# Diagonal scan: product and rounded count on ScalarE, the difference alone on GpSimd

## The reference

```python
mag = jnp.exp(dt * ar)
abar_r, abar_i = mag * jnp.cos(dt * ai), mag * jnp.sin(dt * ai)
...
drive_r = jnp.einsum('bsgh,gph->bsgp', ug, bbar_r)
drive_i = jnp.einsum('bsgh,gph->bsgp', ug, bbar_i)
a_shape = (1, seq, S5_GROUPS, S5_STATE)
elems = (jnp.broadcast_to(abar_r, a_shape), jnp.broadcast_to(abar_i, a_shape), drive_r, drive_i)
_, _, h_r, h_i = lax.associative_scan(_complex_linear_combine, elems, axis=1)
y = (jnp.einsum('bsgp,ghp->bsgh', h_r, c_re.astype(f32))
     - jnp.einsum('bsgp,ghp->bsgh', h_i, c_im.astype(f32)))
```

## Time and profile before

| | |
|---|---|
| median of the runs | 1574.51 us |
| lowest run | 1571.92 us |
| the profiled execution | 1572.47 us, of which the span is 1570.7 us |
| VectorE busy over the span | 1142.6 us, 73% |
| ScalarE busy over the span | 791.3 us, 50% |
| GpSimd busy over the span | 83.2 us, 5%, nearly all of it in the S5 phases |
| S5 phases on GpSimd | 966.5 to 1039.8 us |
| S5 tables on ScalarE | 977.5 to 1072.7 us |
| S5 on VectorE | 977.8 to 1087.6 us |

### The profile page before, as it was taken

The page is one execution under the profiler, slowest core; times in us unless marked ns, Lnnn a source line. Parts: engine busy times, 40 slices in busy tenths (PEclk is TensorE's granted clock), DMA queues, the critical chain, the costliest instruction groups (busy, mean ns, idle before and its releaser), DMA issues.

```text
span 1570.7 us, 22351 instructions
## 1 busy us (share of the span) xinstructions
PE 1467.8 (93%) x8907; PEld 1262.3 (80%) x8910; DVE 1142.6 (73%) x1824; ACT 791.3 (50%) x1079; POOL 83.2 (5%) x82
## 2 busy tenths in 40 slices
PE   5789988999999999999999999889999899999998
PEld 5788765799988889877899888656786578799987
DVE  6798865699876857766886558999985665466653
ACT  4766654455434545444555436547554634354442
POOL 0000000000000000000000003930020000000000
PEclk8999999999999999999999999999999899999999
DMA  9756622678687543336566565333334243245551
GB/s 381 299 202 272 237 101 101 226 297 349 246 340 296 202 161 134 135 122 232 189 239 240 181 217 190 112 108 131 133 134 161 81 161 108 101 161 183 185 195 62
DMA packets 42519, 298.57 MB, mean 190 GB/s; under 512 B 4657, under 2 KB 4913, under 8 KB 7473
## 3 DMA queue, kind: packets, MB, share of 16 engines
q1 hardware_dynamic: 39984, 283.52, 48.6%
q0 software_dynamic: 1568, 8.39, 1.5%
q10 hardware_dynamic: 864, 5.24, 0.9%
HBM read 292.94 MB, written 4.19 MB: 189 GB/s over the span
## 4 chain that ended last, share of the span: by engine, by line
PE 45%; DVE 21%; PEld 15%; ACT 8%; issue 7%; DMA 3%; PEldq 1%; ACTq 0%; SPq 0%; DVEq 0%
PE ps L1038 19%; PE ps L1046 14%; PEld ps L1038 8%; PEld ps L1046 6%; DVE ring_at_lo L1316 6%; ACT w_hi L1305 3%; DMA ring_at<-stream 3%; DVE ring_at L1175 2%; PE ps L1079 2%; PE ps L2626 1%; DVE arena_at L2194 1%; DVE arena_at L3193 1%; PE ps L3096 1%; PE ps L3537 1%; DVE arena_at L3202 1%
## 5 line engine op out<-in xcount | busy, mean ns | idle before, releaser
L1316 DVE TENSOR_TENSOR ring_at_lo<-ring_at,w_hi 128x2048 fp32r<-128x2048 f32 (+1 forms) x218 | 495.9, 2278 | 171.7 <-ACT w_hi L1305 171.2
L1305 ACT ACTIVATE w_hi<-ring_at 128x2048 fp32r<-128x2048 f32 (+1 forms) x218 | 412.3, 1898 | 176.5 <-PE ps L1038 121.1
L1038 PE MATMUL ps<-w_hi,arena_at_lo 128*128 128x512 f32 x1104 | 301.0, 395 | 1.6 <-DVEq L4488 0.8
L1046 PE MATMUL ps<-h_hi,w_hi 128*128 128x256 f32 x1440 | 238.9, 288 | 17.8 <-DVE ring_at_lo L1316 8.3
L1038 PEld LDWEIGHTS ps<-w_hi,arena_at_lo 128*128 128x128 f32 x1104 | 204.8, 188 | 46.1 <-issue 2.7
L1046 PE MATMUL ps<-h_hi,ring_at_lo 128*128 128x256 f32 x1440 | 229.6, 281 | 0.0
L1046 PE MATMUL ps<-hT_at_lo,w_hi 128*128 128x256 f32 x1440 | 229.6, 281 | 0.0
L1046 PEld LDWEIGHTS ps<-h_hi,w_hi 128*128 128x128 f32 x1440 | 199.6, 191 | 26.1 <-issue 16.1
L1046 PEld LDWEIGHTS ps<-hT_at_lo,w_hi 128*128 128x128 f32 x1440 | 196.7, 190 | 0.0
L1046 PEld LDWEIGHTS ps<-h_hi,ring_at_lo 128*128 128x128 f32 x1440 | 196.6, 190 | 0.0
L1038 PE MATMUL ps<-ring_at_lo,arena_at_lo 128*128 128x512 f32 x552 | 170.6, 390 | 0.0
(11 more groups left out here) (464 smaller groups left out, 1646.9 us busy)
## 6 DMA issues: line engine op xcount, KB each, us to landing
ring_at<-stream SPq DMA_DIRECT2D x266, 1024.0 KB, 4.9
arena_at_lo<-kept_hi POOLq DMA_DIRECT2D x4, 1024.0 KB, 7.3
arena_at<-bias ACTq DMA_DIRECT2D x4, 768.0 KB, 6.5
kept<-arena_at POOLq DMA_DIRECT2D x4, 512.0 KB, 4.2
arena_at<-kept ACTq DMA_DIRECT2D x2, 1024.0 KB, 5.8
x_res<-x SPq DMA_DIRECT2D x1, 1024.0 KB, 11.3
arena_at<-mem POOLq DMA_DIRECT2D x1, 1024.0 KB, 12.9
kept_hi<-arena_at_lo POOLq DMA_DIRECT2D x1, 1024.0 KB, 5.1
```

The lines of the kernel that those rows point to most:

```text
L1038: mm = pe.matmul(k.ps[:, bank + t, :], x_tile(f, slice(t * P, (t + 1) * P)), w, start=first and n == 0, stop=last and n == 2)
L1046: mm = pe.matmul(k.ps[:, bank + q // 2, (q % 2) * TOK:(q % 2 + 1) * TOK], w[:, q * P:(q + 1) * P], x, start=first and n == 0 and q % 2 == ...
L1305: act.activation(k.w_hi[:, s % HI, 0:n, :], k.ring[:, c % RING, 0:n, :], ACT.Identity).then_inc(k.hi_done, 1)
L1316: dve.tensor_tensor(k.w_lo[:, c % RING, 0:n, :], k.ring[:, c % RING, 0:n, :], k.w_hi[:, s % HI, 0:n, :].bitcast(F32), ALU.subtract).then_i ...
```

## The change

ScalarE makes the product and the rounded count of a tile by three activations and the new function `counts`: time times turns, the same plus ROUND, and that minus ROUND. The constant ROUND comes as a per-partition operand from two new columns of the constants. GpSimd only takes the difference. `counts(0)` and `counts(1)` come before `tables(0)`, `counts(2)` after it; then `counts(i + 3)` follows `tables(i + 1)` in each step. `n` gets a second buffer, and the waits go by new semaphore counts: GpSimd waits for a tile's three counts, ScalarE for the difference two tiles back before it writes `n` again, and `tables(i)` for difference i.

```diff
+        "rounds": np.broadcast_to([1.5 * 2.0 ** 23, -1.5 * 2.0 ** 23], (P, 2)),
...
-            ("s5_phases", 4 * S5T), ("s5_tables", S5T), ...
+            ("s5_counts", 3 * S5T), ("s5_phases", S5T), ("s5_tables", S5T), ...
...
         def tables(i):
             cos, sn = self.cos[:, i % 3, :], self.sn[:, i % 3, :]
-            act.wait_ge(*m["s5_phases"].at(4 * i + 4))
+            act.wait_ge(*m["s5_phases"].at(i + 1))
...
+        def counts(i):
+            n, r, f = self.n[:, i % 2, :], self.r[:, i % 6, :], self.turns[:, i:i + 1]
+            if i >= 2:
+                act.wait_ge(*m["s5_phases"].at(i - 1))
+            act.activation(r, k.con("time"), ACT.Identity, scale=f).then_inc(m["s5_counts"].sem, 1)
+            act.activation(n, k.con("time"), ACT.Identity, scale=f, bias=k.con("rounds")[:, 0:1]).then_inc(m["s5_counts"].sem, 1)
+            act.wait_ge(*m["s5_counts"].at(3 * i + 2))
+            act.activation(n, n, ACT.Identity, bias=k.con("rounds")[:, 1:2]).then_inc(m["s5_counts"].sem, 1)
+
+        counts(0)
+        counts(1)
         tables(0)
+        counts(2)
         yield
         for i in range(S5T + 3):
             if i + 1 < S5T:
                 tables(i + 1)
+            if i + 3 < S5T:
+                counts(i + 3)
             yield
...
         def phases(i):
-            n, r, f = self.n, self.r[:, i % 6, :], self.turns[:, i:i + 1]
-            if i >= 1:
-                pool.wait_ge(*m["s5_phases"].at(4 * i))
-            if i >= 6:
-                pool.wait_ge(*m["s5_tables"].at(i - 5))
-            pool.tensor_scalar(n, k.con("time"), f, ROUND, ALU.mult, ALU.add).then_inc(m["s5_phases"].sem, 1)
-            pool.tensor_scalar(r, k.con("time"), f, 1.0, ALU.mult, ALU.mult).then_inc(m["s5_phases"].sem, 1)
-            pool.wait_ge(*m["s5_phases"].at(4 * i + 2))
-            pool.tensor_scalar(n, n, 1.0, -ROUND, ALU.mult, ALU.add).then_inc(m["s5_phases"].sem, 1)
-            pool.wait_ge(*m["s5_phases"].at(4 * i + 3))
+            n, r = self.n[:, i % 2, :], self.r[:, i % 6, :]
+            pool.wait_ge(*m["s5_counts"].at(3 * i + 3))
             pool.tensor_tensor(r, r, n, ALU.subtract).then_inc(m["s5_phases"].sem, 1)
...
-    n, r, cos, sn = gla.take(1, TOK)[:, 0, :], gla.take(6, TOK), gla.take(3, TOK), gla.take(3, 2 * TOK)
+    n, r, cos, sn = gla.take(2, TOK), gla.take(6, TOK), gla.take(3, TOK), gla.take(3, 2 * TOK)
```

More of the change, by code:

```diff
@@ L3060, in __init__ @@
         self.m = {n: k.mark(n, c) for n, c in (
-            ("s5_phases", 4 * S5T), ("s5_tables", S5T), ("s5_drive", S5T), ("s5_turned_in", 2 * S5T), ("s5_added_in", S5T),
+            ("s5_counts", 3 * S5T), ("s5_phases", S5T), ("s5_tables", S5T), ("s5_drive", S5T), ("s5_turned_in", 2 * S5T), ("s5_added_in", S5T),
             ("s5_scanned", 2 * S5T), ("s5_turned_out", 2 * S5T), ("s5_c_spread", 4),
```

## The result

The changed kernel takes 1583.97 us in the median of six runs (1578.47 to 1585.27), the kernel before 1570.44 in six runs beside it: a ratio of 1.0084 with a 95% interval of [1.0063, 1.0105]. One of those six was a slow run of 1822.68 us, which the ratio leaves out. Run once more the changed kernel gave 1.0072 [1.0052, 1.0092]. By the ratios it is 11 to 13 us slower; its time lies above the forecast (1573 to 1578) and 1 us above the top of the whole range (1583). The profiled execution took 1584.38 us with a span of 1582.6.

A forecast was written before the change was run, and what follows sets the result against it. VectorE was taken as the bound in the scan (966 to 1090 us). Start +2.7, later place +1.4, clock +0.3, contention -4.0 and subtraction +2.4 make +2.8 us: 1575.5 us forecast, 1573 to 1578 at 0.60, whole range 1570 to 1583.

The forecast's parts named there:

- Elsewhere: Outside the scan's terms: second buffer of `n`, two more constant columns in a load long done, GpSimd's dropped wait; all free.
- Start: Scan's start: counts ahead of the high halves (L1305) delay L1316 and the product of 998.88; +2.7 us, bounds 1.5 and 3.5.
- One later L1305: The L1305 of 1018.16 has only 0.09 us of cover before its L1316; +1.4 us, bounds 0 and 2.9.
- rival 3: ScalarE becomes the bound, L1305 exposed behind every tile's counts: +32 us, 1604 us, over 2% slower; chance 0.02.
- Clock: Scan's output products: both slow ones get about half a microsecond more idle time, +0.3 us.
- the third: Third output product, 1.92 us after 2.88 us idle: falling to 1.2 GHz would cost 1.7 us.
- Contention won: VectorE's scans, turn-outs and sums after 1007 us run faster without three GpSimd instructions per tile; -4.0 us.
- the subtraction kept: GpSimd's subtraction meets VectorE on about 8 later tiles at 0.3 us each; +2.4 us, bounds 0 and 5.3.
- Rival 2: The kept subtraction costs most of what the other GpSimd instructions did: +9.4 us, 1581.9 us; chance 0.14.
- Rival 1: Small gain: subtraction falls beside L1316 or PSUM readers and costs nothing, L1305 of 1018 finds cover; 1571.2 us; chance 0.24.
- the sum by the rule: SBUF port rule: each of 8 kept subtractions costs its whole 0.72 us, 5.8 us instead of 2.4, time 1578.7 us.

The follow-up runs named there:

- padded execution: Profiled run of the changed kernel with 56 unused words ahead of `w_hi`, restoring buffer places within 256 bytes; against the kernel before 1.0031 (1577.64 us).
- mended start: Changed kernel with the first three tiles' product and count left on GpSimd: 1.0049 without pad, 0.9991 with the 56-word pad, against the kernel before.
- padded constants: Kernel before with only the two constant columns and 56 unused words ahead of `w_hi`: 1.0006 [0.9990, 1.0023], 1574.26 us.
- no difference: Changed kernel with the 56-word pad, GpSimd's subtraction left out and `tables` waiting for the counts: 0.9990 [0.9975, 1.0005] against the kernel before, 1571.95 us.
- ScalarE's part alone: Padded kernel, ScalarE's three activations per tile written to an unread buffer, GpSimd doing all four instructions as before: 1.0020 [1.0003, 1.0036], 1575.36 us.
- only the others moved: Kernel before with `w_hi` in place and `h_hi`, `ones` and a small buffer 32 bytes later: 0.9994 [0.9980, 1.0007], 1571.88 us.
- either mending alone: Padded changed kernel with either the first three tiles' counts on GpSimd (0.9991) or the subtraction left out (0.9990), against the kernel before.
- both mendings and pad: Changed kernel with 56-word pad, first three tiles' counts on GpSimd, and counts(i + 3) ahead of tables(i + 1): 0.9984 against the kernel before, 1571.22 us.

## Why the prediction was wrong, step by step

**The step that failed: "Elsewhere ... the constants two more columns in a load long done ... Free".** I costed the columns as a transfer. As a shift of what lies behind them they cost 0.48% [0.30, 0.65] alone, and 0.06% [-0.10, 0.23] with the places restored. Without them the change is at 1.0031, 1577.6 us against 1572.1, inside the range. I had not looked at what lies behind the constants. The prediction also held that only 2%, 31 us, can be told from no change; the intervals here reach some 0.2% to either side.

**The scan's own sum, +2.8 us.** By medians it measured +4.9 us [2.7, 7.2], which includes the forecast. The places of the padded execution, counted from the L1316 of 966.50 to behind the last output product, add up to +6.2 (2.6 + 0.5 - 0.9 + 1.4 - 1.0 + 1.1 + 2.6, within 0.1); I go by those for the terms. That execution is the slowest of its twelve.

*Start, forecast +2.7.* Right. The high halves came 4.3 and 7.2 us late (4.35 and 7.2 forecast) once the 4.17 us are taken off by which ScalarE's instruction just ahead of the counts (975.57 before, 979.74 after) was late already. The first output product came 2.6 us late, with and without pad. What I missed is the first step: `tables(0)` stands behind two counts too, so the first turn-in already waited 2.49 us at 986.61, and the wait at L1317 behind it was shorter for that. From the L1317 of 998.30 to the product VectorE won back 0.6 us (0.75 forecast). The mended start confirms the place: 0.40% less with pad, 0.23% less without.

*One later L1305, forecast +1.4.* Right. L1317 of 1027.88 waits 1.69 us, and the difference grows by 1.4 us there. No other chunk was exposed, so rival 3 is out.

*Clock, forecast +0.3.* From the first output product to the turn-in behind it the difference grew by 0.45 us with pad (0.2 without), and the second row's product takes 3.51 instead of 3.30 us: some 0.65 for both. But the third, which I priced at 1.7 us and left out of the sum, fell and cost 2.6: 1.7 by itself, the rest on the products behind it. This is the largest miss in the scan. It had 3.7 us of idle time before it in the changed kernel, with and without pad. Yet even 2.9 us is followed now by the one clock, now by the other. Here is the same product in the kernel with the padded constants, with no difference, with ScalarE's part alone, and with the constants alone:

```profile
1065.46 1.92 PE L3098 MATMUL ps<-arena_at 128*32 128x256 f32 x16 [2.88 <-DVE arena_at L3204]
```

```profile
1067.25 3.06 PE L3098 MATMUL ps<-arena_at 128*32 128x256 f32 x16 [2.88 <-DVE arena_at L3207]
```

```profile
1071.91 2.83 PE L3098 MATMUL ps<-arena_at 128*32 128x256 f32 x16 [2.88 <-DVE arena_at L3219]
```

```profile
1068.31 3.63 PE L3097 MATMUL ps<-arena_at 128*32 128x256 f32 x16 [2.91 <-DVE arena_at L3203]
```

After the same 2.9 us the product runs at 2.4 GHz in the first and, as before, in the earlier trace rows; in the others it is longer, up to the 3.63 us of 1.2 GHz. It also took 2.90 us with `w_hi` moved and 3.30 with only the others moved. Five of the profiled kernels have the scan unchanged (before, constants alone, padded constants, and these two), and their stretch from 966.50 on differs from that of the profiled kernel before by 0, 2.7, -0.1, 2.5 and 1.8 us, nearly all of it at the slow output products. Their mean is 1.4, and 6.2 less 1.4 is 4.8, near the medians' 4.9. That such chance explains the gap between the two is likely, but each of the five was profiled once, so it isn't shown.

*Contention won, -4.0, and the subtraction kept, +2.4.* The win was right: behind the first output product the scans, the sums and the turn-outs took 4.1 us more than undisturbed ones before. The eight later meetings were counted right too. The size of one was wrong, 0.43 us and not 0.3: the subtraction kept cost VectorE 3.4 us there (with pad) instead of 2.4, so 0.7 was left of the 1.6 that I had as the gain. And the instruction was wrong: it is the scans, not the turn-outs, that it meets. First the kernel before from 980 to 1095 us (busy us, mean ns), the scan first, then L3202, L3184 and L3200:

```profile
L3193 DVE TENSOR_TENSOR_SCAN arena_at<-arena_at 128x256 f32<-128x256 f32 x32 | 22.9, 754 | 0.1
L3202 DVE TENSOR_TENSOR arena_at<-arena_at 128x512 f32<-128x512 f32 x16 | 13.3, 831 | 0.0
L3184 DVE TENSOR_TENSOR arena_at<-arena_at 128x512 f32<-128x512 f32 x16 | 12.2, 763 | 0.0
L3200 DVE TENSOR_TENSOR arena_at<-arena_at 128x512 f32<-128x512 f32 x16 | 11.8, 741 | 0.0
```

The padded changed kernel (L3208 and L3210 are the turn-outs, L3192 the sum), and then the one without the difference (L3205, L3207 and L3189):

```profile
L3201 DVE TENSOR_TENSOR_SCAN arena_at<-arena_at 128x256 f32<-128x256 f32 x32 | 24.4, 804 | 0.1
L3208 DVE TENSOR_TENSOR arena_at<-arena_at 128x512 f32<-128x512 f32 x16 | 11.2, 699 | 0.0
...
L3210 DVE TENSOR_TENSOR arena_at<-arena_at 128x512 f32<-128x512 f32 x16 | 10.9, 681 | 0.0
...
L3192 DVE TENSOR_TENSOR arena_at<-arena_at 128x512 f32<-128x512 f32 x16 | 10.6, 664 | 0.0
```

```profile
L3198 DVE TENSOR_TENSOR_SCAN arena_at<-arena_at 128x256 f32<-128x256 f32 x32 | 20.2, 674 | 0.1
...
L3207 DVE TENSOR_TENSOR arena_at<-arena_at 128x512 f32<-128x512 f32 x16 | 11.0, 685 | 0.0
L3205 DVE TENSOR_TENSOR arena_at<-arena_at 128x512 f32<-128x512 f32 x16 | 11.0, 685 | 0.0
...
L3189 DVE TENSOR_TENSOR arena_at<-arena_at 128x512 f32<-128x512 f32 x16 | 10.7, 668 | 0.0
```

The four groups take 60.2 us before, 57.1 with the subtraction alone and 52.9 without it. The scans got slower (754 to 804 ns) while the rest got fast; without the subtraction they take 674. I wrote that scans would take 673 to 720 and L3202 around 0.8 us: it was the other way round.

The end saw this: in the padded execution the difference falls by 0.9 us before the late L1305 and by 1.0 after it, and then grows by 1.1 in the stretch that was clean before, 0.8 us less in all where I had 1.6. VectorE's turn-in also waits longer for TensorE's drive product, 6.0 us (6.5 with pad) instead of 2.4, in the same four places. Most of that is the clock again: at the fourth place, behind the third of the slow products, the wait went from 0.5 to 3.0 us. At the first it went from 0.6 to 1.8 us (2.1 with pad), since TensorE, late from the start, makes the next drive late. "A little of it lies where VectorE would then wait for TensorE", 0.2 us in my sum, was too small a discount for that place.

*Rivals.* Rival 2 named a price, 1581.9, near the measured 1583.97, but by luck: over half of the measured cost is the constants', which it doesn't have. Of its own terms one came true, the third product that fell; the start was not at its upper bound, and no second L1305 was late. One subtraction cost 0.43 and not 0.53 us. Rival 1 failed: the L1305 of 1018 found no cover.

**Still open.** Why the starting place of `w_hi` matters, and where 3 to 4 of its 7.5 us lie. Whether the scan's own cost is 2.8 or 4.9 us, since the interval holds both, and how much of the third product's fall is the change's doing. Why either mending alone takes the whole cost away. Whether the kernel with both mendings and pad (0.9984 [0.9967, 1.0001]) beats the kernel before: it beats the changed one, but from before and from the mended start alone (0.9991) it can't be told apart.

## What to carry to other kernels

A new constant or a wider buffer can move what is allocated behind it: price the places before the operations, and run the new layout alone, then the change with its old places restored by a pad. In an engine that works in order, put new work inside a wait that the trace shows (counts ahead of `tables`), and keep it off the start, where nothing is yet ahead of it that could cover it. A term that is priced but left out of the sum, like the third product here, needs a share of its own in the sum when its rows lie near those that fell. And a stretch read from one profiled execution carries that execution's chance: here up to 2.7 us with nothing in it changed.

## What the runs showed of the hardware

*The place of an operand.* Moving the fp32r buffer `w_hi` by 32 bytes per partition, from 64 to 96 bytes within a block of 256, took the distance of 512-column products from 229.9 to 231.6 ns and ScalarE's write of a 128x2048 half from 1910 to 1914 ns. Products with `ring_at_lo` and `arena_at_lo`, neither of which moved, slowed from 390 to 393 ns, while those with `w_hi` and `h_hi` went from 397 to 395. No mechanism for this was shown.

*Who pays in a meeting.* A subtraction on GpSimd beside a pair of scans, in GpSimd's timeline after:

```profile
993.19 1.21 POOL L3157 TENSOR_TENSOR arena_at<-arena_at 128x256 f32<-128x256 f32 x1 [3.96 <-ACT arena_at L3134]
...
1002.17 0.72 POOL L3157 TENSOR_TENSOR arena_at<-arena_at 128x256 f32<-128x256 f32 x1 [4.83 <-ACT arena_at L3134]
...
1038.84 3.34 POOL L3157 TENSOR_TENSOR arena_at<-arena_at 128x256 f32<-128x256 f32 x1 [6.35 <-ACT arena_at L3134]
```

The pair of 993.20 took 1.75 us instead of 1.26 and the subtraction 1.21 instead of 0.72: each lost 0.49 us. Singly, the first scan took its 0.68 us, and the second 1.15. The row of 1038.84 starts beside the turn-out L3209 of 1038.70 and then lies beside L1317 of 1039.31; neither was stretched (0.68 and 2.28 us), and all 2.6 us went to GpSimd. The Trainium skill, SBUF — State Buffer, section "SBUF: two separate sides", has the one that comes second wait for the other's end. These rows agree in kind: the subtraction waits for the first scan, the second scan for the subtraction. But a meeting cost VectorE 0.43 us in the mean of eight, not 0.72, so the sum by the rule (5.8 us) was too high and mine (2.4) too low: 3.4 was measured.
